# A seven-product SwiGLU: VectorE adds the third and fourth banks of a pair of weight tiles before, not after, the first two sums of the next pair's weights

## The reference, cut to what matters

```python
def _swiglu(h, w1, w3, w2):
    return (jax.nn.silu(h @ w1) * (h @ w3)) @ w2

x = _residual(x, _swiglu(_modnorm(x, ...), ffn1_w1, ffn1_w3, ffn1_w2), ...)      # x 512 rows, ctx 256 rows
...
x = _residual(x, _swiglu(_modnorm(x, ...), ffn2_w1, ffn2_w3, ffn2_w2), ...)      # x 512 rows
```

## Time and profile before

| | |
|---|---|
| median of 3 runs | 2315.57 us (2314.34 to 2315.95) |
| the profiled execution's own time | 2315.04 us |
| its span in the profile | 2313.2 us |
| PE busy | 2250.8 us, 97% of the span |
| VectorE busy | 1307.3 us, 57% |
| GpSimd busy | 1291.5 us, 56% |
| ScalarE busy | 963.2 us, 42% |
| TensorE clock granted, mean | 0.997 |

### The profile page before, as it was taken

One profiled execution on the slowest core, in us unless ns is written; L12 is line 12 of the kernel. 1 busy time (PEld: TensorE's weight loads), 2 busy tenths in 40 slices (PEclk: granted clock), 3 DMA queues, 4 the chain that ended last, 5 costly groups with the idle time before them and its releaser, 6 DMA issues.

```text
span 2313.2 us, 35228 instructions
## 1 busy us (share of the span) xinstructions
PE 2250.8 (97%) x12694; PEld 1937.2 (84%) x12694; DVE 1307.3 (57%) x2094; ACT 963.2 (42%) x1500; POOL 1291.5 (56%) x1448
## 2 busy tenths in 40 slices
PE   7999999999999999999999999999999999999997
PEld 6778787678888889999999979877766887999997
DVE  3324632598878778464554563343137556876666
ACT  4454544544233454332332342355435535444433
POOL 3434465099878766564544533322446064977775
PEclk9999999999999999999999999999999999999999
DMA  4222232356555542222212212222230031323232
GB/s 160 89 82 75 72 119 94 110 175 200 194 196 192 193 129 74 73 73 66 72 64 73 75 55 97 80 71 80 82 89 27 1 109 64 101 92 110 92 110 74
DMA packets 68241, 230.54 MB, mean 100 GB/s; under 512 B 7296, under 2 KB 12672, under 8 KB 67968
## 3 DMA queue, kind: packets, MB, share of 16 engines
q1 hardware_dynamic: 51232, 177.92, 23.2%
q10 hardware_dynamic: 16864, 50.60, 6.6%
HBM read 225.61 MB, written 2.10 MB: 98 GB/s over the span
## 4 chain that ended last, share of the span: by engine, by line
PE 74%; issue 9%; DVE 9%; POOL 5%; ACT 3%; DMA 0%; POOLq 0%; DVEq 0%; ACTq 0%; SPq 0%
PE ps L2290 18%; PE ps L2796 11%; PE ps L2294 9%; PE ps L2851 6%; PE ps L2855 6%; PE ps L2852 6%; POOL WLO L443 5%; PE ps L2999 4%; PE ps L2346 2%; PE ps L2301 1%; PE ps L2941 1%; PE ps L2970 1%; PE ps L2984 1%; PE ps L3138 1%; PE ps L3121 1%
## 5 line engine op out<-in xcount | busy, mean ns | idle before, releaser
L443 POOL TENSOR_TENSOR WLO<-RAW,WHI 128x256 fp32r<-128x256 f32 x1004 | 867.6, 898 | 740.5 <-ACT WHI L542 739.6
L542 ACT ACTIVATE WHI<-RAW 128x1024 fp32r<-128x1024 f32 x251 | 262.9, 1056 | 290.2 <-DMA RAW<-in_stream_dram 282.4
L462 POOL TENSOR_TENSOR WLO<-RAW,WHI 128x256 fp32r<-128x256 f32 x240 | 227.5, 969 | 205.7 <-DVE SRAW L1913 85.7
L2290 PE MATMUL ps<-HLO,WHI 128*128 128x512 f32 (+2 forms) x872 | 317.4, 380 | 0.0
L2290 PE MATMUL ps<-HHI,WHI 128*128 128x512 f32 (+2 forms) x872 | 309.9, 371 | 0.0
L2294 PE MATMUL ps<-HHI,WLO 128*128 128x512 f32 (+2 forms) x872 | 198.4, 371 | 0.3 <-POOL WLO L443 0.3
L2290 PEld LDWEIGHTS ps<-HLO,WHI 128*128 128x128 f32 (+1 forms) x872 | 159.4, 188 | 33.4 <-issue 4.0
L2290 PEld LDWEIGHTS ps<-HHI,WHI 128*128 128x128 f32 (+1 forms) x872 | 159.4, 188 | 31.9 <-issue 3.3
L2294 PEld LDWEIGHTS ps<-HHI,WLO 128*128 128x128 f32 (+1 forms) x872 | 153.9, 188 | 29.2 <-POOL WLO L443 0.5
L2796 PE MATMUL ps<-GLO,WHI 128*128 128x384 f32 (+1 forms) x480 | 143.7, 353 | 1.2 <-POOL WLO L443 1.1
L2851 PE MATMUL ps<-HLO,WHI 128*128 128x384 f32 (+1 forms) x480 | 141.1, 310 | 3.5 <-DVE SF L1946 3.5
(11 more groups left out here) (507 smaller groups left out, 5364.6 us busy)
## 6 DMA issues: line engine op xcount, KB each, us to landing
RAW<-in_stream_dram SPq DMA_DIRECT2D x331, 512.0 KB, 3.3
ADA<-in_ada_dram ACTq DMA_DIRECT2D x72, 512.0 KB, 4.3
BM<-in_bias_dram ACTq DMA_DIRECT2D x8, 448.0 KB, 3.7
DECAY<-in_decay_dram ACTq DMA_DIRECT2D x4, 512.0 KB, 4.2
C<-in_ctx_dram ACTq DMA_DIRECT2D x2, 1024.0 KB, 5.5
out_dram<-X SPq DMA_DIRECT2D x16, 128.0 KB, 1.8
X<-in_x_dram SPq DMA_DIRECT2D x2, 512.0 KB, 5.8
X<-in_x_dram ACTq DMA_DIRECT2D x2, 512.0 KB, 6.7
```

The source lines that it names most:

```text
L443: op = nc.gpsimd.tensor_tensor(WLO[:, slot(u), k:k + 2], RAW[:, slot(u), k:k + 2], WHI[:, slot(u), k:k + 2].bitcast(F32), ALU.subtract)
L462: op = nc.gpsimd.tensor_tensor(WLO[:, j, k:k + 2], RAW[:, j, k:k + 2], WHI[:, j, k:k + 2].bitcast(F32), ALU.subtract)
L542: nc.scalar.activation(WHI[:, j], RAW[:, j], ACT.Copy).then_inc(unit_hi, 1)
L2290: nc.tensor.matmul(out, high[k], x[:, k, tok], start=(k == 0 and n == 0), stop=False)
```

## The change

VectorE's `upper(p)` is put ahead of `first_sums(p+1)`. In the first three pairs of each group the two sums L1913 and L1915 of the next pair so run after L1949 in place of before L1943. In the fourth pair nothing changes. No instruction is added or taken away, and no other engine's order differs.

```diff
--- before.py
+++ after.py
@@ -1979,9 +1979,9 @@
                     dve.wait_ge(s("coef"), len(COEFS))
                 for p in range(PAIRS):
                     c = p // 4 + 1
+                    upper(z, p)
                     if p % 4 < 3:
                         first_sums(z, p + 1)
-                    upper(z, p)
                     if p % 4 < 3:
                         last_sums(z, p + 1)
                         last_lows(z, p + 1)
```

## The result

The changed kernel takes 2324.51 us, the median of five executions, against 2315.61 us for the kernel before on the same chips: 1.0038 times as long, with a 95% interval of 1.0026 to 1.0049. It is slower by 8.9 us; 2325.1 us and +9.5 us were forecast. One of the five ran at a granted clock of 0.643 and took 3255.86 us; the others took 2321.56 to 2328.49 us, and the ratio is theirs. The profiled execution took 2321.56 us and has a span of 2319.8 us, 6.6 us more than before. It is the shortest of the runs: it enters the second network 2.2 us earlier than the execution before (1977.83 against 1980.03 us), a difference ahead of everything that the change touches there and that the sum doesn't contain. What makes them differ stays open.

A forecast was written before the change was run, and what follows sets the result against it. The prediction took PE as the bound, fully busy in the first network and waiting eight times for L1946 in the second. Terms -5.5 + 15.0 + 0 = +9.5 us on 2315.57 us gave 2325.1 us, range 2314 to 2329 us.

The forecast's parts named there:

- the sum: Whole kernel: -5.5 us for waits removed, +15.0 us for new waits, 0 in the first network, together +9.5 us.
- Eight waits for L1946 go: Second network: with L1913 and L1915 no longer ahead of L1943 to L1949, PE's eight waits for L1946 vanish, -5.5 us.
- The chain from product 4 to the end of the fourth L462: Second network, pair ends: from product 4's start through VectorE's steps to GpSimd's fourth L462 ending, 6.06 us.
- From GpSimd to PE: Second network, pair ends: from the end of GpSimd's fourth L462 to PE's start, 0.15 us, making 6.21 us.
- 15 of them: Second network: a new 1.0 us PE wait for product 0's low part, three pair ends in five groups, +15.0 us.
- First network 0 us: First network, 15 pair ends: low part ready after at most 6.4 us, wanted after 7.63 us, so no cost.
- No new wait: Rival, second network: fourth L462 ends before 5.13 us, only the 5.5 us gain is left, 2310.1 us; chance 0.12.
- Half of it: Rival, second network: one sum slowed or GpSimd's third instruction ahead of L1925; 15 x 0.6 us, +3.5 us, 2319.1 us; chance 0.15.
- The first network didn't join: Rival: first network meets GpSimd oftener and waits 0.3 us at 15 pair ends, 4.5 us on top, 2329.6 us; chance 0.06.
- the first rival: The rival "No new wait": product 0's low part in time, only the 5.5 us gain left, 2310.1 us; chance 0.12.

## Why the prediction was right

- **Eight waits for L1946 go, -5.5 us.** Right: none is left, and the groups of before had lost 5.6 us.
- **The chain from product 4 to the end of the fourth L462, 6.06 us.** Right: 6.04 us. The starts come out at 0.27 us (L1949), 0.60 (L1913), 1.32 (L1915), 1.93 (L1923), 3.19 (L1925), 4.23 (L1932) and 5.38 us (L1936), where the prediction's steps add up to 0.27, 0.61, 1.33, 1.94, 3.20, 4.23 and 5.38 us. Each was taken from another place of the trace, where the same two kinds of instructions followed one another.
- **From GpSimd to PE, 0.15 us.** Too much: 0.05 us. The row of before was from another pair of lines, L443 and L2346. This is the term that was mis-sized; with the right one the same sum gives 0.92 in place of 1.0 us.
- **15 of them.** Right; one of them cost 1.09 us, most others 0.9 us. 13.9 us in place of 15.0 us, and with it +8.3 us in the groups, where the sum had +9.5 us. The medians differ by 8.9 us, and the interval (6 to 11 us) holds both. That they come within 0.6 us of the forecast is in part luck: the groups give 1.2 us less than the sum.
- **First network 0 us.** Right, by the run that changed only this network: 1.0000, with 6.20 us needed where the prediction had at most 6.4 us.
- **The rivals.** No new wait was to be had only with the fourth L462 before 5.13 us; it ended at 6.04 us. Half of it fell with L1925 at 1.12 us. The first network didn't join. The run without GpSimd's first two L462 shows what the first rival would have been: 0.9984, 5.5 us less in the groups.
- **What the prediction had wrong without a price.** It paid the slowness of L1913 and L1915 in the kernel before to GpSimd without naming the instruction, and its only rows of GpSimd are of L462 and L443. They meet L467 and L470, the tail of the pair before. The sum used only what a meeting costs and where it falls after the change, so this did no harm there, but it made two expectations fail (the one without the first two L462 on the order of before, and the exchange of GpSimd's steps). It also reads L1932's 1.23 us as one L1932 alone and half of an L462 step; by its rows that would be 0.69 + 0.70 = 1.39 us. The sum took starts from the trace and didn't use it.

Why another order alone hardly helps, as an estimate: GpSimd has ten instructions a pair, VectorE eight that read two SBUF tiles (L1913, L1915, L1923, L1925, L1932, L1936, L1960, L1962). Slowed by each other they take about 0.55 us and 0.6 us apiece of common time: a 128x512 of VectorE adds 0.61 us from start to start (L1915 to L1923), a GpSimd instruction adds 0.54 us to the one it meets. 8 x 0.6 + 10 x 0.55 = 10.3 us, an estimate from these rows, against PE's 10.08 us for a pair. By this estimate the two engines can't be clear of one another unless GpSimd's turns fall beside VectorE's bank steps or its idle time. No run shows that no order does it, and the estimate alone doesn't tell a good kernel: without GpSimd's two L462 it comes to 9.2 us, and the order of before still lost 5.1 us in its groups. Where the meeting falls matters too, and the changed order puts it on the chain to product 0's low part.

The Trainium skill, page "SBUF — State Buffer", section "SBUF: two separate sides", says that a VectorE instruction with two SBUF inputs and a GpSimd instruction that reads SBUF lock each other out of the ports for a whole instruction. The runs agree in the main: beside a GpSimd instruction of 256 columns such an instruction took 1.23 us, beside one of 512 columns 1.78 us, and with one input in a bank 0.41 to 0.43 us in any company. But not quite the whole length is paid: the shortest L462 of 256 columns takes 0.72 us and added 0.54 us, the shortest of 512 columns 1.28 us and added 1.09 us.

## What to carry to other kernels

Before moving VectorE's instructions, write down which of them read two SBUF tiles and which read a bank, and put the bank readers where GpSimd's instructions run; a sum moved away from behind a wait of its own may land on GpSimd's turn, ahead of a result that PE wants. If VectorE and GpSimd together fill the period, moving a meeting only moves the wait: take an instruction out of the turns instead, for instance by leaving an operand in a bank. Here that gave 0.9983 on the order of before, and nothing on the changed order, whose wait hung on another stretch. And read the chain to the next wait step by step from neighbouring rows, with the margin at its end (5.28 us wanted, 6.04 us needed): here that told nearly every wait to 0.1 us. A list of waits can leave short ones out; the distance of starts has them.

## What the runs showed of the hardware

- The price of a meeting grows with GpSimd's instruction: 128x512 on VectorE went from 0.69 to 1.23 us beside 128x256 on GpSimd, and to 1.78 us beside 128x512. Whether it depends on VectorE's length too, no run here tells. Making GpSimd's steps half as many and twice as long cost 0.6% on top of the changed order. All forty executions of the first slowed sum (L1924) in that kernel, in ns:

```profile
L1924 DVE TENSOR_TENSOR SRAW<-SRAW,RAW x40: 684/1783/1791, 896.0 to 2279.9; 128x512 f32<-128x512 f32 x40
```

- The turns seem to alternate, one instruction of VectorE and one of GpSimd, where both have work ready. In the longer kernel L1926 took 0.69 us between two of 1.78 us, since GpSimd, which had been idle for 0.63 us until L1924 ended, started its next one just after it (2123.54 against 2123.49 us).
- VectorE writes the sum of a bank and a tile into a bank in 0.43 us, as fast as into a tile (0.42 us), and reading it back keeps the next instruction out of the turns:

```profile
2119.24 0.43 DVE L1949 TENSOR_TENSOR ps<-SF,ps 128x256 f32<-128x256 f32 x1
```
